# Block one of a two-block network: root mean squares applied after the linear groups, two tickets per PSUM bank, sums of squares in 32-column strips

## The reference, cut to what matters

```
h = rmsnorm(x, norm_attn)              # y = x * rsqrt(mean(x*x) + eps) * g
proj = h @ w_in                        # queries, keys, values of 16 heads in four kinds of attention
x = x + mixed @ w_out                  # mixed: the heads' outputs
h2 = rmsnorm(x, norm_mlp)
x = x + square(relu(h2 @ w_up)) @ w_down
```

## Time and profile before

| | |
|---|---|
| Median of three runs | 2387.3 us (2383.19 to 2387.49) |
| Profiled execution | 2387.66 us, span 2385.9 us |
| PE busy | 2269.5 us, 95% |
| DVE busy | 1354.4 us, 57% |
| ACT busy | 1200.3 us, 50% |
| Mean granted clock of PE | 0.994 |
| 256- and 512-column matmuls at L731 | 9648, 1572.6 us |

### The profile page before, as it was taken

The page is one execution under the profiler, slowest core; times in us unless marked ns, Lnnn a source line. Parts: engine busy times, 40 slices in busy tenths (PEclk is TensorE's granted clock), DMA queues, the critical chain, the costliest instruction groups (busy, mean ns, idle before and its releaser), DMA issues.

```text
span 2385.9 us, 33877 instructions
## 1 busy us (share of the span) xinstructions
PE 2269.5 (95%) x13594; PEld 1875.0 (79%) x13594; DVE 1354.4 (57%) x2320; ACT 1200.3 (50%) x2115; POOL 12.2 (1%) x10
## 2 busy tenths in 40 slices
PE   8999999999999999999999999999999998899998
PEld 8759999957999777787676676867777876669898
DVE  6665655565665655445556564366656345546664
ACT  4655544555554563444344342356555236446654
POOL 0000000000000000000000000000000000000000
PEclk9999999999999999999999999999999999999999
DMA  8863544793455213222121121222222222214443
GB/s 299 319 244 142 178 176 167 262 368 122 172 176 183 90 70 106 89 88 99 45 87 64 60 89 36 90 70 96 97 89 89 106 71 89 88 56 142 168 149 107
DMA packets 45721, 312.30 MB, mean 131 GB/s; under 512 B 4951, under 2 KB 7255, under 8 KB 8580
## 3 DMA queue, kind: packets, MB, share of 16 engines
q1 hardware_dynamic: 45572, 310.20, 36.0%
HBM read 309.11 MB, written 1.07 MB: 130 GB/s over the span
## 4 chain that ended last, share of the span: by engine, by line
PE 80%; DVE 9%; ACT 7%; issue 2%; DMA 1%; SPq 0%; ACTq 0%; DVEq 0%
PE bank L731 55%; PE bank L736 8%; DVE ws L1601 3%; ACT ws L1173 2%; PE bank L906 2%; PE bank L1064 2%; DVE xs L1617 2%; PE bank L814 1%; PE bank L967 1%; PE bank L1035 1%; PE bank L803 1%; PE bank L892 1%; PE bank L891 1%; PE bank L948 1%; ACT xs L1189 1%
## 5 line engine op out<-in xcount | busy, mean ns | idle before, releaser
L731 PE MATMUL bank<-xs,ws 128*128 128x256 f32 (+1 forms) x9648 | 1572.6, 324 | 70.1 <-DVE xs L1617 48.4
L731 PEld LDWEIGHTS bank<-xs,ws 128*128 128x128 f32 x9648 | 1402.1, 192 | 243.8 <-DVE xs L1617 67.1
L1601 DVE TENSOR_TENSOR ws<-ring,ws 128x1024 fp32r<-128x1024 f32 x464 | 551.1, 1229 | 303.5 <-ACT ws L1173 303.0
L1173 ACT ACTIVATE ws<-ring 128x1024 fp32r<-128x1024 f32 x464 | 464.7, 1050 | 298.2 <-PE bank L731 278.5
L1617 DVE TENSOR_TENSOR xs<-arena,xs 128x512 fp32r<-128x512 f32 (+1 forms) x286 | 167.0, 600 | 304.2 <-ACT xs L1189 303.3
L1189 ACT ACTIVATE xs<-arena 128x512 fp32r<-128x512 f32 (+1 forms) x286 | 149.0, 539 | 339.1 <-PE bank L731 224.5
L1617 DVE TENSOR_TENSOR xs<-hT,xs 128x256 fp32r<-128x256 f32 (+1 forms) x328 | 178.2, 552 | 191.6 <-ACT xs L1189 191.6
L1189 ACT ACTIVATE xs<-hT 128x256 fp32r<-128x256 f32 (+1 forms) x328 | 165.7, 518 | 221.3 <-PE bank L731 189.6
L736 PE MATMUL bank<-ws,xs 128*128 128x512 f32 (+1 forms) x1008 | 230.1, 388 | 9.3 <-DVE xs L1617 5.1
L736 PEld LDWEIGHTS bank<-ws,xs 128*128 128x128 f32 x1008 | 188.5, 189 | 49.7 <-DVE xs L1617 6.4
L803 PE MATMUL bank<-con 128*128 128x256 f32 x224 | 51.3, 380 | 2.2 <-DVE arena L2104 2.2
(11 more groups left out here) (253 smaller groups left out, 1474.6 us busy)
## 6 DMA issues: line engine op xcount, KB each, us to landing
ring<-in_stream SPq DMA_DIRECT2D x233, 1024.0 KB, 4.8
arena<-in_side SPq DMA_DIRECT2D x56, 1024.0 KB, 6.0
arena<-bias_vectors SPq DMA_DIRECT2D x1, 1536.0 KB, 7.8
hT<-in_tokens SPq DMA_DIRECT2D x1, 1024.0 KB, 5.7
arena<-in_tokens SPq DMA_DIRECT2D x1, 1024.0 KB, 13.1
out<-arena SPq DMA_DIRECT2D x2, 512.0 KB, 3.1
arena<-in_params SPq DMA_DIRECT2D x1, 918.0 KB, 8.8
arena<-bias_vectors SPq DMA_DIRECT2D x1, 706.0 KB, 9.3
```

Of the source, the lines that this page charges most:

```text
L731: ins = mm(ps(n, 0, g.T), a[wi][:, p * P:(p + 1) * P], x[xi], start=first, stop=last)
L1173: do(ws[:, i % 2, 0, c], ring[:, w % R, c], ACT.Copy).then_inc(w_high, 1)
L1601: ins = v.tensor_tensor(ws[:, i % 2, 1, c], ring[:, w % R, c], ws[:, i % 2, 0, c].bitcast(F32), ALU.subtract)
```

## The change

1. The groups of proj, nat and up take x times the gain as input (ACT by a scale operand, DVE by a fused multiply and subtract) instead of the normed `hT`. The root is applied to their results: by DVE for proj (`scaled`), in DVE's relu for up (square then on ACT, two buffers of 512 columns), and as a per-token scale in ACT's copies for nat, for which PE turns the root into a column (ticket `rT`).
2. Two tickets share a bank in proj, out, up and down: columns 0 to 255 and 256 to 511, released at the second. Adds, squares and copies take 512 columns.
3. The sum of squares is taken in four groups of 32 columns (`group_sums`), copied by ACT and summed and spread by a second product (`spread_sum`). Both stand inside the next group, after its third and fourth chunk.
4. The warming products ahead of proj (layer 1), up and down are gone; at the start and ahead of m_up they are regrouped.
5. Down's first two chunks are split ahead of up 3's results. The eight half copies of proj 1 stand behind nat's third chunk. The context half of the first modulation stands ahead of down's last residual.
6. On SP, parameters go ahead of slot 0; the bias vectors are read back behind slot 5; the side loads are spread over the slots up to out.

```diff
 class Group / stream_plan / ticket_plan
+        w.group(("proj", l, i), 8, KD, T, "x", pair=True, gain=("g_attn", l))
+        w.group(("nat", l), 4, KD, T, "x", natural=True, gain=("g_attn", l))
+        w.group(("up", l, i), 8, KD, T, "x", pair=True, gain=("g_mlp", l))
...
 PE, linear: (n, c) = place(g, p) is bank ticket and first column
-                            first, last = k == i == 0, k == g.K - 1 and i == 2
+                            first, last = k == i == c == 0, k == g.K - 1 and i == 2 and (c > 0 or not g.pair)
-                                ins = mm(ps(n, 0, g.T), a[wi][:, p * P:(p + 1) * P], x[xi], start=first, stop=last)
+                                ins = mm(ps(n, c, c + g.T), a[wi][:, p * P:(p + 1) * P], x[xi], start=first, stop=last)
...
+            def group_sums(i):
+                n = N(("sq", i))
+                pe.wait_ge(bank_free[n % BANKS], n // BANKS)
+                for j in range(2):
+                    pe.wait_ge(sq_ready, seen(sq_ready, 2))
+                    for c in range(4):
+                        ins = mm(bank[n % BANKS][32 * c:32 * c + 32, 0:T], ones[:, 0:32], act[:, 4 * j + c, :],
+                                 start=(j == 0), stop=(j == 1))
+                ins.then_inc(bank_full[n % BANKS], 1)
+            def spread_sum(i):
...
+                mm(ps(n, 0, T), con[:, CON("sums") + 2:CON("sums") + 3].to_broadcast([P, P]), relu[:, 1, 0:T],
+                   start=True, stop=True).then_inc(bank_full[n % BANKS], 1)
-                sum_squares(N(("rms1", l)), lambda k: act[:, k, :], KD, T, ones, True)
-                keep_warm(N(("proj", l, 0)), T, T, 4 if l else 3)
+                linear(G("proj", l, 0), 0, 3)
+                group_sums(2 * l)
+                linear(G("proj", l, 0), 3, 4)
+                spread_sum(2 * l)
+                linear(G("proj", l, 0), 4, 6)
+                n = N(("rT", l))
+                pe.wait_ge(rstd_ready, seen(rstd_ready))
+                for t in range(2):
+                    ins = mm(ps(n, t, t + 1), stat[:, 0, t * P:(t + 1) * P], ident[:, 0:1], start=True, stop=True)
+                linear(G("proj", l, 0), 6)
...
-                keep_warm(N(("down", l)), T, T, 3)
+            group_sums(2 * DEPTH)
+            keep_warm(N(("m_up", 0)), T, T, 2)
+            spread_sum(2 * DEPTH)
+            keep_warm(N(("m_up", 0)), T, T, 7)
 ACT
+            def sums_within(i, g):
+                feed_to(g.q0 + 4)
+                group_sums_out(i)
+                feed_to(g.q0 + 5)
+                rstd(N(("rms", i)), T, D)
...
+                g = G("up", l, 0)
+                feed_to(g.q0)
+                pair_squares(("out", l), 0)
+                feed_to(g.q0 + 2)
+                for j in range(1, 4):
+                    pair_squares(("out", l), j)
+                sums_within(2 * l + 1, g)
                 for i in range(4):
                     g = G("up", l, i)
-                    feed(g, int(i < 3))
+                    feed(g, 1 if i < 3 else 2)
+                    for j in range(4):
+                        n = N(g.name) + j
+                        act_.wait_ge(bank_free[n % BANKS], n // BANKS + 1)
+                        do(act[:, 8 * i + 2 * j:8 * i + 2 * j + 2, :], relu[:, j % 2, :]..., ACT.Square).then_inc(act_ready, 1)
 DVE
+            def residual(name, g):
+                for j in range(4):
+                    n = N(name) + j
+                    dve.wait_ge(bank_full[n % BANKS], n // BANKS + 1)
+                    v.tensor_tensor(rows_of(xT, j), rows_of(xT, j), pair_of(n), ALU.add).then_inc(bank_free[n % BANKS], 1)
+                    if j == 1 and g:
+                        feed_to(g.q0)
...
+                    feed(g, 1 if i < 3 else 2)
+                    if i == 0:
+                        dve.wait_ge(rstd_ready, seen(rstd_ready))
+                    for j in range(4):
+                        n, done = N(g.name) + j, 16 * l + 4 * i + j
+                        dve.wait_ge(bank_full[n % BANKS], n // BANKS + 1)
+                        if done % 16 >= 2:
+                            dve.wait_ge(act_ready, done - 1)
+                        stt(relu[:, j % 2, :]..., pair_of(n), 0.0, scaled_by(stat), ALU.max, ALU.mult).then_inc(bank_free[n % BANKS], 1)
...
+            for k in range(KD):
+                modulate_part(k, 0)
+            residual(("down", DEPTH - 1), None)
             dve.wait_ge(rstd_ready, seen(rstd_ready))
 SP
-            for i in range(2):
-                load(R + i)
             sp.wait_ge(bank_free[N("bias") % BANKS], N("bias") // BANKS + 1)
             sp.dma_start(scratch, relu[0:12, 0, :]).then_inc(dma_bv, 16)
+            for i in range(4):
+                load(R + i)
             sp.wait_ge(dma_bv, 16)
```

More of the change, by code:

```diff
@@ L172, in consts_layout @@
     p.add("ones", 128)
+    p.add("sums", 3)
     p.add("rope", 256)
@@ L176, in consts_layout @@
     p.add("strips", 2 * ADA_B)
-    p.add("sums", 2)
     return p
@@ L188, with __init__ @@
 class Group:
-    def __init__(self, name, tickets, K, T_, src, natural=False, fresh=None):
-        self.fresh = fresh
+    def __init__(self, name, tickets, K, T_, src, natural=False, fresh=None, pair=False, gain=None):
+        self.fresh, self.pair, self.gain = fresh, pair, gain
         self.name, self.tickets, self.K, self.T, self.src, self.natural = name, tickets, K, T_, src, natural
@@ L273, in ticket_plan @@
     n = Tickets()
-    n.add("xT", KD)
+    n.add("xT", KD // 2)
+    n.add("bias")
     for l in range(DEPTH):
-        n.add(("rms1", l))
-        if l == 0:
-            n.add("bias")
-        for i in range(2):
-            n.add(("proj", l, i), 8)
+        n.add(("proj", l, 0), 4)
+        n.add(("sq", 2 * l))
+        n.add(("rms", 2 * l))
+        n.add(("rT", l))
+        n.add(("proj", l, 1), 4)
         n.add(("nat", l), 4)
@@ L304, in ticket_plan @@
         n.add(("dfn", l))
-        n.add(("out", l), 8)
-        n.add(("rms2", l))
-        for i in range(4):
-            n.add(("up", l, i), 8)
-        n.add(("down", l), 8)
-    n.add("rmsf")
+        n.add(("out", l), 4)
+        n.add(("up", l, 0), 4)
+        n.add(("sq", 2 * l + 1))
+        n.add(("rms", 2 * l + 1))
+        for i in range(1, 4):
+            n.add(("up", l, i), 4)
+        n.add(("down", l), 4)
+    n.add(("sq", 2 * DEPTH))
+    n.add(("rms", 2 * DEPTH))
     for i in range(4):
@@ new lines, in _ @@
+            keep_warm(N(("proj", 0, 0)), T, T, 3)
+            n = N("bias")
+            pe.wait_ge(dma_par1, 16)
+            pe.wait_ge(dma_oh, 16)
+            mm(bank[n % BANKS][0:12, :], par1[0:33, PAR1("table"):PAR1("table") + 12], oh, start=True, stop=True).then_inc(bank_full[n % BANKS], 1)
+            keep_warm(N(("proj", 0, 0)), T, T, 5)
+            def group_sums(i):
[6 more added lines that the diff above has]
+                                 start=(j == 0), stop=(j == 1))
+                ins.then_inc(bank_full[n % BANKS], 1)
@@ L837, in _ @@
+                linear(G("proj", l, 1))
                 linear(G("nat", l), 0, 6)
@@ L1536, in _ @@
             for half in range(2):
-                scale_residual(6, LAT, half)
+                scale_residual(2, LAT, half)
             feed(G("a_uq", 0), 1)
```

284 lines of the change are left out of this document (153 added, 131 removed).

## The result

The changed kernel takes 2373.7 us, the median of five executions (2370.8 to 2376.2), against 2387.3 before (2383.2 to 2387.5): ratio 0.9946, interval 0.9933 to 0.9958. It is faster by 13.6 us, about 0.55%, where 10.7 had been forecast (2376.6). The profiled execution takes 2374.29 us around a span of 2372.4.

A forecast was written before the change was run, and what follows sets the result against it. TensorE is busy 95% of the span, so only seams where it lacks useful matmuls can pay. Terms -9.2 - 4.2 + 1.6 + 0 + 3.6 - 3.2 + 0 + 0.7 = -10.7 give 2376.6 us; range 2369 to 2386.

The forecast's parts named there:

- Out to up, and up to up: Block one seams: out to up gains 4.6 us, twice (-9.2); up to up is 0.27 late, six times (+1.6).
- Up to down: Seam into down, both layers: 2.1 us late against 2.13 before, moved by two chunks; no gain, PE idle without warming.
- Down to proj: Seam from down to proj: like out to up, plus products turning the root into a column; gain 4.2 us.
- Natural group: Natural group in each layer: lateness 2.2 becomes 0.4, attention's start loses 0.2; -1.6 us per layer, -3.2 in all.
- Start: Kernel start through proj 1: later bias reads make DVE 1.2 us late instead of 2.29; taken as 0, bounds -1.6 and +2.
- Down to the second block: Seam after last down: modulations ahead of the residual put first scale 1.95 us later, 1.25 comes back; +0.7.
- Two tickets per bank: Rival, proj, out, up, down: alternating bank halves slows matmuls; 5 ns each costs 21 us, giving 2397.7; chance 0.08.
- The rule on drains: Strips of the group sums: tiling-mode switches drain TensorE; by the rule 1.7 us worse, but rows were followed instead.
- The clock there: Idle wait at up to down: PE's clock falls to 1.2 GHz, costing 1.8 us, twice; +3.6, bounds 0 and 3.6.
- The steps without the clock: All forecast terms from start to second block except the +3.6 us for clock falls at up to down.
- The rival in which the clock holds: Rival at up to down: no clock fall behind the waits, so 3.6 us less, 2373.0 us; chance 0.24.

The follow-up runs named there:

- the second profile: The changed kernel run again with nothing edited; 2375.4 us, ratio 0.9960 to the kernel before.
- the slot experiment: Against the changed kernel, ACT and DVE drain up's last four pairs before splitting down's second weight slot; 2373.0 us, ratio 0.9948.
- the full-width run: Against the changed kernel, sums of squares as eight full-width products into one bank, without strips, copy or spreading product; 2384.7 us, ratio 0.9994.
- the third: The changed kernel run a third time with nothing edited; 2376.3 us, ratio 0.9954 to the kernel before.

## Why the prediction was right, step by step

- *Out to up, and up to up.* From the start of out to the third chunk of down it is 129.53 us before (183.14 to 306.90 + 48 x 0.1203) and 125.70 after (182.06 to 307.76), in layer two 125.71. That is 3.83 less, where 4.6 less three times 0.27 had been stepped: 3.8. Inside it two small errors cancel: strips and spread put off the next matmul by 1.1 and 0.25 us, 1.4 for the 1.6 put down, and the wait ahead of the third chunk, 2.10 and the 0.17 that rows overlap, is 2.27 late for the 2.13 of before. The three handovers cost 0.9 together (720 matmuls behind the spread take 87.53, the dense 720 of down 86.62), 0.3 each.
- *Up to down.* 2.1 late, moved by two chunks: 2.10 in both layers. The cause stepped, the second slot ahead of the drain, is what the slot experiment took away.
- *Down to proj.* From the third chunk of down to the natural group it was 138.8 us (312.67 to 405.31 + 384 x 0.1203 = 451.5); the second profile, without a fall there, has 307.43 to 442.03, 134.6. Forecast 4.2, measured 4.2.
- *Natural group.* This term came out too large. Its 1.6 a layer had 0.2 for the start of attention taken off already, so it counts to the first product of attention:

```profile
92.82 0.46 PE L891 MATMUL bank<-arena 64*128 64x128 f32 x2 [0.72 <-DVE arena L1699]
...
451.46 2.62 PE L736 MATMUL bank<-ws,xs 128*128 128x512 f32 x12
...
478.55 0.46 PE L891 MATMUL bank<-arena 64*128 64x128 f32 x2 [0.72 <-DVE arena L1699]
```

These are lines of the kernel before. In the first layer it is 27.07 us there (65.75 to 92.82) and 26.07 after (65.67 to 91.74), in the second 27.09 and 25.86 (443.88 to 469.74). That is 1.0 and 1.2 less, 2.2 for the 3.2 put down. Inside the group 1.3 and 1.6 are won, and the wait ahead of attention takes 0.3 back (0.99 and 1.08 for 0.72).
- *Start.* Forecast 0; the natural group's start is 65.67 and 65.26 in two profiles, against 65.75 and 64.14 in the two of before. The mechanism is shown (the bias reads were late, by 1.4 to 1.7 of idle time against 1.2 forecast); the size lies inside the scatter of the start.
- *Down to the second block.* The forecast put the first scale 1.95 later and the first product 1.95 - 0.33 = 1.62, with 0.93 back in the two waits. From the end of down to the first product it is 7.27 before and 9.10 after where the clock held, 1.83 lost, and the waits give 1.27 back: 0.6 lost for 0.7. The move alone, by the run that takes it back, costs 1.72 and gives 0.92.
- *Two tickets per bank* was the rival on the other side. 264 matmuls in 31.94 us less the overlap of 0.17 are 0.1203 each, as before: nothing is lost.
- The rule on drains (the Trainium skill, TensorEngine Tiling (Array Packing), Key Properties) had been left out of the sum, and the rows bear that out: the set of strips takes 1.00 us to the next matmul (213.94 to 214.94 in the first layer), as in attention, and the row ahead of it overlaps it by 0.06, where rows overlap by 0.17 otherwise: about 0.1 us lost there, which the sum had. The strips' own worth is shown by the full-width run.
- *The clock there* is the other step that was mis-sized. It took a fall behind each of the two waits for certain and put +3.6 into the sum; the rows it rested on held five falls after seven idle stretches over 2 us. It passed over that two more falls in the same trace stand behind idle stretches of 1.44 us (2183.92 and 2262.69), so that the length alone does not sort them. In the first profile both waits fell, 3.4 us of clock time and 3.0 in the rows. But over the nine profiles of kernels that keep the wait, 9 of 18 such waits are followed by a fall: both in the first profile, neither in the second, one in the third. So the mean of the term is half of what was put down, 1.7 of clock time and 1.5 in the rows. That the wait is what lets the clock fall there is borne out, though six are few, by the three kernels that fill or remove it: none of their six passages is followed by a fall.

The steps without the clock sum to -14.3 in the forecast. Measured one by one they are 2 x 3.83 + 4.19 + 2.23 - 1.83 + 1.27 = 13.52 us, and what is missing is the natural group. At equal clock the runs show 13.1, which agrees with 13.5 within the errors and the scatter of the start; with the 1.2 that the lower mean clock takes back that is 11.9, between the forecast and the first five executions. So the forecast stood near because the natural group's gain was put too large and the clock's cost too large as well, which cancels in part.

The difference of 13.5 in the spans of the two profiles has three parts: 13.5 by the steps as measured and 0.1 at the start, 4.4 against it for the three falls ahead of the second block (two rows and the last seam are 1.5, 1.5 and 1.4 longer than in the profiles without them), and 4.3 for it in the second block, which goes with the scatter of the falls. The forecast took the first two (with 14.3 and 3.6) and could not have the third. That the 4.3 nearly makes up for the 4.4 is luck; the first five executions, at a mean clock of 0.9946 where all sixteen of the changed kernel have 0.9937, share some of it. The rival in which the clock holds, 2373.0, comes near the measured time, though in the profile shown the clock did not hold at all; that nearness is chance.

Open: what decides whether a given wait is followed by a fall, and whether the changed kernel's lower mean clock (0.9937 against 0.9944, means of values given to 0.001, a difference within its 95% error of 0.0008) is a cost of PE idling where warming products stood before. No run takes back the two tickets per bank or the new order in the natural group by itself, so their part is read from rows only.

## What to carry to other kernels

A norm's root that commutes with the product costs no waiting on the path, only the 1.4 us of its own products, once both its sums and its use stand behind a few chunks of the next group; each half of that (not waiting for the squares, not waiting for the root) has to be done, at 3.2 and 2.9 us a seam here. Ahead of a drain, look at what the two splitting engines have queued: a look-ahead of weights made the 2.1 us wait that was left in each layer. When the clock of PE scatters, compare landmarks with the falls taken out, or times at equal mean clock: that resolved effects of 1.5 to 2 us which medians of five executions could not. Times at equal clock leave out what an edit does to the clock itself.

## What the runs showed of the hardware

- The same 2.10 us of idle time, in the same place of the same program, is followed by the lower clock in some executions and not in others; a fall costs about 1.7 us of clock time, and in a few places 3.4 in one stretch (470 to 477 us in the second profile of the changed kernel, in attention, behind 1.08 us of idle time). The wait of 3.46 us near 1980 us goes with a fall in all fourteen profiles. In the run that waits for the root both idle stretches of 2.53 us kept the clock, while both of 2.10 in the same execution lost it:

```profile
220.00:222.00 2.00, 0.89 (x7) 0.90 (x8) 2.00 (x3) 1.82 (x5) 0.00 (x0) 1.00 0.00 0
222.00:224.00 2.00, 2.00 (x19) 2.00 (x18) 0.48 (x2) 0.00 (x0) 0.00 (x0) 1.00 0.42 115
...
310.00:312.00 2.00, 1.32 (x11) 1.35 (x12) 1.47 (x3) 2.00 (x4) 0.00 (x0) 1.00 0.34 139
312.00:314.00 2.00, 2.00 (x11) 2.00 (x11) 2.00 (x4) 0.82 (x3) 0.00 (x0) 0.51 0.00 0
```

 The Trainium skill, TensorE: Matmul & The Clock Gate, section "The HAM clock gate", says that the monitor behind the clock runs free of the program, so that the moment of a change varies from run to run. That agrees with these rows; the experiments did not test it by itself.
- Eight products of 256 float32 columns take 3.62 us at full width and 1.07 in four groups of 32 output columns.
- Two groups of columns of one bank, written in turn by three matmuls each, run at the same 0.1203 us a matmul as one bank for each (264 in 31.94 us, less the overlap of 0.17).
